# A fourth weight sum moved from VectorE to an accumulating DMA out of SBUF, with one eviction and one save issued earlier

## The reference

```
h = _layernorm(ALPHA * h + mix, ln1_g[l], ln1_b[l])
ff = (jax.nn.silu(h @ w_ffn_gate[l]) * (h @ w_ffn_up[l])) @ w_ffn_down[l]
h = _layernorm(ALPHA * h + ff, ln2_g[l], ln2_b[l])
```

## Time and profile before

| | us |
|---|---|
| median of 3 runs (1746.59 to 1748.63) | 1747.46 |
| the profiled execution, its own time | 1745.96 |
| its span in the profile | 1744.3 |
| PE busy | 1722.5 |
| DVE busy | 1186.7 |
| ACT busy | 831.7 |
| POOL busy | 95.0 |

### The profile page before, as it was taken

The page is one execution under the profiler, slowest core; times in us unless marked ns, Lnnn a source line. Parts: engine busy times, 40 slices in busy tenths (PEclk is TensorE's granted clock), DMA queues, the critical chain, the costliest instruction groups (busy, mean ns, idle before and its releaser), DMA issues. The chain is left out here.

```text
span 1744.3 us, 19544 instructions
## 1 busy us (share of the span) xinstructions
PE 1722.5 (99%) x8292; PEld 1447.7 (83%) x8292; DVE 1186.7 (68%) x998; ACT 831.7 (48%) x680; POOL 95.0 (5%) x87
## 2 busy tenths in 40 slices
PE   9999999999999999999999998999999999999999
PEld 8888888998888888888887886887878787888886
DVE  5765656677775745444676777888888897855545
ACT  5454544454444445444444625455545455554332
POOL 0000002222121300000000000000000000000000
PEclk9999999999999999999999998999999999999999
DMA  9667655454445556746888948777887886878553
GB/s 345 252 238 223 211 189 179 163 184 169 162 169 177 169 191 239 257 169 234 262 269 248 377 134 260 237 240 223 262 233 244 239 248 171 258 240 303 195 193 126
DMA packets 121329, 387.36 MB, mean 222 GB/s; under 512 B 8608, under 2 KB 43808, under 8 KB 102688
## 3 DMA queue, kind: packets, MB, share of 16 engines
q1 hardware_dynamic: 112384, 364.56, 62.0%
q0 software_dynamic: 2720, 10.49, 3.1%
q10 hardware_dynamic: 6144, 11.14, 1.7%
HBM read 359.82 MB, written 25.69 MB: 221 GB/s over the span
## 5 line engine op out<-in xcount | busy, mean ns | idle before, releaser
L1263 DVE TENSOR_TENSOR weight_lo<-raw,weight_hi 128x2048 fp32r<-128x2048 f32 x213 | 489.0, 2298 | 376.2 <-ACT weight_hi L879 374.6
L879 ACT ACTIVATE weight_hi<-raw 128x2048 fp32r<-128x2048 f32 x213 | 408.2, 1916 | 532.5 <-DMA raw<-in_stream 532.4
L1978 PE MATMUL pair<-weight_hi,act_both 128*128 128x512 f32 x672 | 268.9, 400 | 9.1 <-DVE weight_lo L1263 9.1
L1980 PE MATMUL pair<-weight_hi,act_both 128*128 128x512 f32 x672 | 262.9, 391 | 0.0
L1979 PE MATMUL pair<-weight_lo,act_both 128*128 128x512 f32 x672 | 262.7, 391 | 0.0
L1952 PE MATMUL pair<-act_both,weight_hi 128*128 128x512 f32 x600 | 211.3, 394 | 0.0
L1163 ACT ACTIVATE part_hi<-part_raw 128x2048 fp32r<-128x2048 f32 x60 | 114.3, 1914 | 161.1 <-DMA part_raw<-in_stream 55.2
L1950 PE MATMUL pair<-act_both,weight_lo 128*128 128x256 f32 x640 | 172.8, 280 | 0.0
L1712 DVE TENSOR_TENSOR part_lo<-part_raw,part_hi 128x2048 fp32r<-128x2048 f32 x60 | 136.8, 2287 | 44.1 <-ACT part_hi L1163 44.1
L1978 PEld LDWEIGHTS pair<-weight_hi,act_both 128*128 128x128 f32 x672 | 126.9, 189 | 36.1 <-DVE weight_lo L1263 7.3
L1980 PEld LDWEIGHTS pair<-weight_hi,act_both 128*128 128x128 f32 x672 | 126.7, 189 | 27.0
(11 more groups left out here) (304 smaller groups left out, 2780.0 us busy)
## 6 DMA issues: line engine op xcount, KB each, us to landing
raw<-in_stream SPq DMA_DIRECT2D x259, 1024.0 KB, 5.3
part_raw<-in_stream SPq DMA_DIRECT2D x30, 1024.0 KB, 7.1
scratch<-spill ACTq DMA_DIRECT2D x40, 256.0 KB, 4.6
part_raw<-in_stream POOLq DMA_DIRECT2D x10, 1024.0 KB, 11.5
ln_rows<-in_ln_rows SPq DMA_DIRECT2D x6, 1024.0 KB, 8.2
gate<-scratch SPq DMA_DIRECT2D x12, 512.0 KB, 6.8
ff_scratch<-ff_blocks SPq DMA_DIRECT2D x11, 512.0 KB, 5.0
ff_land<-ff_scratch SPq DMA_DIRECT2D x44, 128.0 KB, 5.2
```

The costliest lines, as they stand in the source:

```text
L879: act.activation(hi_of(n), raw_of(n), ACT.Copy).then_inc(extra_h if extra(n) else h_ready, 1)
L1263: dve.tensor_tensor(lo_of(n), raw_of(n), hi_of(n).bitcast(F32), ALU.subtract)\
L1978: pe.matmul(out, hi[:, k0 + k, tok], w_hi[:, k, :], start=first and k == 0, stop=False)
L1980: mm = pe.matmul(out, lo[:, k0 + k, tok], w_hi[:, k, :], start=False, stop=last and k == 3)
```

## The change

Three things are done.

The fourth sum leaves DVE. SP loads the quadrant G a second time, straight into W_H (`load_fourth`), and POOL then issues a DMA that adds F to it, out of SBUF into SBUF. It waits for F (`part_sum`) and for that load (`fourth_in`), and signals `fourth_sum`. As F's low half is written over F, DVE's low half of F (products 4 and 10) now waits for `fourth_sum`. `sum_t4` is gone.

In ACT's order `take_gate(p, 0)` stands ahead of `part_split(p, 8)`.

The save of the second half of z is issued ahead of the load of piece n+6; before, it stood behind plain 0. The load of part A of block 0 moves behind piece n+6.

```diff
         def part_ready(eng, p, j):
             w, s = WEIGHT[j], j // 6 if j < 12 else 1
-            first = 3 * (2 * p + s)
+            first = 2 * (2 * p + s)
...
             elif w == W_H:
-                eng.wait_ge(part_sum, first + 3)
+                eng.wait_ge(fourth_sum, 16 * (2 * p + s + 1))
...
+            def load_fourth(p, s):
+                if 2 * p + s:
+                    sp.wait_ge(part_used, PRODUCTS * p + 6 if s else PRODUCTS * p)
+                sp.dma_start(part_of(W_H).rearrange("p (h c) -> p h c", h=2), ffn_part(2 * p + 1, 1, 2 + s))\
+                    .then_inc(fourth_in, 16)
...
             sp.wait_ge(h_done, 16)
+            sp.dma_start(h_scratch[P:T, :], z[:, 1, :]).then_inc(z_out, 16)
+            loads(first + 6, first + 7)
             load_part(0, 0, W_A)
-            loads(first + 6, first + 8)
+            loads(first + 7, first + 8)
             sp.wait_ge(piece_used, first + 5)
             load_plain(0, 0)
-            sp.dma_start(h_scratch[P:T, :], z[:, 1, :]).then_inc(z_out, 16)
...
             sp.wait_ge(piece_used, first + 8)
+            load_fourth(0, 0)
             load_part(0, 0, W_G0)
             load_part(0, 1, W_G1)
...
                 load_part(p, 1, W_A)
+                if p:
+                    load_fourth(p, 0)
                 load_plain(p, 3)
...
                 load_plain(p, 5)
+                load_fourth(p, 1)
                 load_plain(p, 6)
...
-                    pool.wait_ge(part_sum, 3 * (2 * p + s) + 1)
+                    pool.wait_ge(part_sum, 2 * (2 * p + s) + 1)
                     pool.dma_start(part_of(W_B).rearrange("p (h c) -> p h c", h=2),
                                    up[2 * p + 2][:, :, s * half:(s + 1) * half], accum_op=ALU.add).then_inc(third_sum, 16)
+                    pool.wait_ge(part_sum, 2 * (2 * p + s) + 2)
+                    pool.wait_ge(fourth_in, 16 * (2 * p + s + 1))
+                    pool.dma_start(part_of(W_H), part_of(W_F), accum_op=ALU.add).then_inc(fourth_sum, 16)
...
                 plain_split(p, 4)
+                take_gate(p, 0)
                 part_split(p, 8)
-                take_gate(p, 0)
                 part_split(p, 9)
...
                 dve.wait_ge(part_h, PRODUCTS * p + j + 1)
                 w = WEIGHT[j]
+                if w == W_F:
+                    dve.wait_ge(fourth_sum, 16 * (2 * p + j // 6 + 1))
...
-            def sum_t4(p, s):
-                w = (W_G0, W_G1)[s]
-                dve.wait_ge(part_in[w], 16 * (p + 1))
-                dve.wait_ge(part_sum, 3 * (2 * p + s) + 2)
-                used(p, s, 6, 14)
-                dve.tensor_tensor(part_of(W_H), part_of(W_F), part_of(w), ALU.add).then_inc(part_sum, 1)
```

More of the change, by code:

```diff
@@ L375, in encoder_program @@
         third_sum = sem("third_sum")
+        fourth_in = sem("fourth_in")
+        fourth_sum = sem("fourth_sum")
         part_h = sem("part_h")
@@ L1736, in sum_t2 @@
                 dve.wait_ge(part_in[W_E], 16 * (2 * p + s + 1))
-                dve.wait_ge(part_sum, 3 * (2 * p + s) + 1)
+                dve.wait_ge(part_sum, 2 * (2 * p + s) + 1)
                 used(p, s, 5, 11)
                 dve.tensor_tensor(part_of(W_F), part_of(W_D), part_of(W_E), ALU.add).then_inc(part_sum, 1)
-            def sum_t4(p, s):
-                w = (W_G0, W_G1)[s]
-                dve.wait_ge(part_in[w], 16 * (p + 1))
-                dve.wait_ge(part_sum, 3 * (2 * p + s) + 2)
-                used(p, s, 6, 14)
-                dve.tensor_tensor(part_of(W_H), part_of(W_F), part_of(w), ALU.add).then_inc(part_sum, 1)
             def take_sums(p):
@@ L1829, in _ @@
                     lo_of_form(F_S2)
-                sum_t4(p, 0)
                 if p:
@@ L1844, in _ @@
                 plain_split(p, 4)
-                sum_t4(p, 1)
                 part_split(p, 8)
```

## The result

The changed kernel takes 1776.49 us (median of 4 runs, 1773.85 to 1778.52), the kernel before 1747.03 (1745.69 to 1748.63). The ratio is 1.0167, with a 95% interval of 1.015 to 1.0185: slower by 29.5 us. I had forecast slower, 1759 with a range of 1732 to 1772, so the sign was right and the size was not: 11.3 us were forecast, and 1776.49 lies outside the range.

The account below looks back on a forecast made before the run. PE, busy for 99% of the span, was taken as the bound, so only its waits count. -9.1 - 5.8 + 17.2 + 6.8 + 2.2 = +11.3 us on the median 1747.46 gave 1759 us, range 1732 to 1772.

Parts of the forecast that it names:

- Part 1: Residual rows ahead of the blocks: saving z earlier brings back nearly all of PE's long wait and slow clock, -9.1 us.
- Part 2: Silu moved ahead of the split of product 8: all four PE waits for it go, -5.8 us.
- Part 3: Ten adds taken off DVE: PE has no wait for DVE in the blocks, so worth nothing by itself.
- Part 4, the first halves: Product 4 of blocks 1 to 4 waits until the accumulate has read F: +4.3 us each, +17.2 us.
- The clock's net price: Slow clock behind the waits at product 4: 1.1 us net a fall, one fall in two, +2.2 us.
- The second halves: DVE, late after its wait at F, delays the third sum and products behind it: +1.7 us a block, +6.8 us.
- A: Rival: the accumulate inside SBUF is quick, 6.5 us or less: -12.5 us, 1735.0 us; chance 0.20.
- B: Rival: the accumulate takes 8.5 us, so no difference: -0.1 us, 1747.4 us; chance 0.15.
- a sign of being wrong: An accumulate from part_raw landing in under 8 us would take the forecast waits away.
- The rule of the Trainium skill: Under it F would be free in time and every wait hidden: -14.9 us, 1732.6 us, the faster end of A.
- C: Rival: the DMA engines become the bound and loads PE needs just in time slip: +21.3 us, 1769 us; chance 0.10.

Follow-up runs that it names:

- e9: Kernel before with only the save of z ahead of piece n+6 and that order of the loads: 1735.7 us, ratio 0.9946.
- e10: Kernel before with only the Silu moved ahead of the split of product 8: 1737.78 us, ratio 0.9957.
- e2: Changed kernel with both moves (save of z, Silu) taken back, the fourth sum still by DMA: 1804.66 us, ratio 1.035.
- e6: Changed kernel without the second loads, POOL copying F plainly into W_H where the accumulate was, so H lacks quadrant G: 1729.18 us, one run.
- e1: Kernel before with the two moves alone (save of z, Silu), the fourth sum still on DVE: 1730.74 us, ratio 0.9911.
- e5: Changed kernel with the second half's load B held back until the first half's fourth sum has landed, blocks 1 to 4: 1761.29 us, ratio 1.008.
- e8: Changed kernel with 26 filler matmuls on PE ahead of product 4 in blocks 1 to 4: 1778.67 us, ratio 1.017.
- e7: Changed kernel with the first halves' fourth sum back on DVE, by DMA in the second halves alone: 1736.86 us, ratio 0.9936.
- e11: On top of e3, the second halves' new load issued behind plain piece 6 and not ahead of it: 1750.55 us, ratio 1.0048.
- e3: Changed kernel with the first halves' new load (blocks 1 to 4) issued 8.7 us earlier, ahead of product 0: 1739.5 us, ratio 0.9969.

## Why the prediction was right in kind and wrong in size

**Part 1** (-9.1) holds: z and the loads behind it landed as estimated (piece n+6's high half began at 1053.94, n+7's at 1060.99; I had 1055.0 and 1060.2), 0.90 us of the wait is left, and e9 measured -9.2.

**Part 2** (-5.8) holds: no Silu wait is left, and e10 measured -7.1. "As long as the third sum is no later than now" wasn't met, and e2 shows how much hangs on it: 18.1 us of Silu waits without the move.

**Part 3** (0) was right as far as it can be seen. e6 leaves the sums off DVE and out of the chain and has 1729.18 us, against e1's 1730.74 with the sums on DVE; the difference is no more than single runs show.

**Part 4, the first halves** is where it failed, by three terms of the sum in the same direction. The mechanism was the forecast one, down to the product, the four blocks and DVE's idle time. The place of the wait was right, its length was 7.6 and not 4.3 us. One: the new load. I let it end one load after A, 12.9 us after product 0 starts; the accumulate went out 14.7 us after (1154.81 to 1169.47). A's own 7.0 us was taken as fixed, though two loads now followed each other where one had; A took 8.6 us and the new load 10.7. Two: the accumulate, 10.8 assumed and 11.6 to 13.1 measured. In block 1 the two terms are 1.8 and 2.3 us, which is the wait of 8.3 us for 4.3. I took the first half's third sum as the nearest row, since it too had two loads beside it, and set 12.3 as the upper bound, though the same rows have one of 14.2. e5 shows that the loads beside it set much of this number: 7.7 to 9.9 us without B. Three: the clock. It was put at one fall in two and fell in four of four; as it fell behind the 3.2 us of e5 too, it would most likely have fallen behind the 4.3 us of the forecast.

**The clock's net price** was put at +1.1 a fall, as DVE catches up while PE is slow. That direction is borne out, and more: in block 1 of e8 and of the changed kernel PE comes to plain 5 as late with its clock as without it (36.3 and 36.4 us behind product 4), so there a fall cost next to nothing on top of DVE's lateness. Of the 18.2 us by which the sum was short (29.5 for 11.3), 13.1 are the length of the waits at product 4 (30.3 for 17.2). Slow clock and second halves together came to 8.1 + 5.6 = 13.7 us for 9.0, another 4.7. The 0.4 left is less than the medians can tell.

**The second halves** (+6.8) were near in size, in part by luck: 5.6 us of waits, and 6.1 us as e7 against e1. The forecast cause was that DVE is late after its wait at F. But e7 has no wait at F in a first half and still 4.2 us of these waits, and e11 removes them by moving the load. The new load beside the third sum makes these; 0.4 us was what I had allowed for it, and third sums in second halves took 13.5 to 14.5 us for 12.3. DVE's lateness is there as well, hidden under the slow clock. From product 4 to plain 5 PE took 13.9 us more than in e1 over blocks 1 to 4 of the changed kernel, and 5.9 us more in e7; the other 8.0 come with the wait at F.

**Rivals.** A and B needed an accumulate of 8.5 us or less. With little beside it, it takes 7.1 us, so A's idea wasn't idle, but there it has loads beside it. Nor would its length have been enough: in block 1 of e5 it landed in 7.7 us, which the forecast names as a sign of being wrong, and PE still waited 3.2 us, since it went out 14.9 us after product 0 and not 12.9. The rule of the Trainium skill, DMA: Bandwidth & Descriptors, section Anatomy of one DMA (about 2.0 us plus the bytes over 436 GB/s, by estimate 4.4 us for 1 MB), is not borne out by any accumulate here: the shortest out of SBUF took 7.1 us. The plain copies of e6, on the same queue, took 7.2 us at best. C as put, the DMA engines as the bound, is refuted by e3, which carries the same traffic at 1739.5 us; but C's mechanism in small, each DMA longer by what stands beside it, is what stretched the accumulate (e5); for the new load, 10.7 us long, the same is argued and not shown. The forecast gave C's price of 1769 a chance of 0.10 and should have treated contention as the likely case, since by its own count 82 of 83 us were full.

## What to carry to other kernels

A sum handed from an engine to the DMA engines costs little by its own work and much by where its chain starts: here the same 20 MB cost 8.8 us over the best kernel with the load issued 5 us ahead of the block, and 45.8 with it behind the block's first load. When a DMA is added where the engines' share is already near 0.8, lengthen every DMA beside it in the estimate, the ones it depends on first, and don't read an upper bound off the longer of two rows. And when a change bundles parts, price the parts apart: the two moves were worth 14.7 us and the third part hid them.

## What the runs showed of the hardware

- An accumulating DMA of 1 MB from SBUF into SBUF lands in 7.1 us with little beside it (the second halves), in 7.7 to 9.9 us with load B held back (e5), in 11.6 to 13.1 us in the first halves of the changed kernel, and in up to 15.8 us beside the next block's loads (e11). The ones from HBM in the blocks took 8.2 us at best over all runs (e11), a plain copy of 1 MB from SBUF into SBUF 7.2 to 10.2 us (e6).
- The clock of PE fell from 2.4 to 1.2 GHz behind every wait of PE in the blocks that lasted 2.88 to 8.3 us (among them 2.88 us in e2, 3.03 us in e8 and 3.2 us in e5), and behind none of up to 1.8 us. Between these the length alone doesn't decide it: it fell behind 2.60 us (e9) and 2.61 us (e8) and not behind 2.58 and 2.85 us (e8). What else does is open. It can fall after the wait has ended: behind the 3.2 us in e5 the first matmuls were at full speed. Look at all matmuls behind a wait and not at the first. Product 4 took 4.2 to 5.3 us behind a fall, for 2.7.
- A lost clock needn't cost time: where another engine is the later one a few us on, keeping PE fast only moved the wait (e8).
